# Gate and up projections of four FFN stages by seven half-width products instead of eight, with the inner layer in four parts

## The reference, cut to what matters

```python
def swiglu_2(x, w_gate_up, w_down):
    g, u = jnp.split(x @ w_gate_up, 2, axis=-1)
    return (jax.nn.silu(g) * u) @ w_down

# for i in range(2), with D_FF_2 = 2816, FFN_RES_SCALE = 0.5:
h = h + FFN_RES_SCALE * swiglu_2(rms_norm(h, ffa_norm[i]), ffa_w_gate_up[i], ffa_w_down[i])
# ... attention ...
h = h + FFN_RES_SCALE * swiglu_2(rms_norm(h, ffb_norm[i]), ffb_w_gate_up[i], ffb_w_down[i])
```

## Time and profile before

| | us |
|---|---|
| three timed runs | 3969.07, 3982.18, 3983.56 |
| median | 3982.18 |
| span of the profiled execution (the page gives no other time of it) | 3971.9 |
| PE busy | 3876.2 (98%) |
| PE weight loads busy | 3199.9 (81%) |
| DVE busy | 2080.0 (52%) |
| ACT busy | 1325.4 (33%) |
| POOL busy | 502.1 (13%) |

### The profile page before, as it was taken

One profiled execution on the slowest core, in us unless ns is written; L12 is line 12 of the kernel. 1 busy time (PEld: TensorE's weight loads), 2 busy tenths in 40 slices (PEclk: granted clock), 3 DMA queues, 4 the chain that ended last, 5 costly groups with the idle time before them and its releaser, 6 DMA issues.

```text
span 3971.9 us, 47501 instructions
## 1 busy us (share of the span) xinstructions
PE 3876.2 (98%) x19522; PEld 3199.9 (81%) x19522; DVE 2080.0 (52%) x3073; ACT 1325.4 (33%) x1977; POOL 502.1 (13%) x526
## 2 busy tenths in 40 slices
PE   8999999999999989999999989999999999999999
PEld 5788988788878878888888867888888888778887
DVE  6636566646459985333443554443643344553345
ACT  3335444322233233223322354322432233342233
POOL 0025551100012220001100143000100000010001
PEclk9999999999999999999999999999999999999999
DMA  6220003545231114233232321232322233022322
GB/s 217 85 70 1 1 1 117 159 138 182 82 101 47 61 40 137 88 104 96 94 101 80 109 64 43 96 101 83 119 87 94 94 98 97 22 64 91 106 89 70
DMA packets 342866, 350.73 MB, mean 88 GB/s; under 512 B 9595, under 2 KB 338107, under 8 KB 342396
## 3 DMA queue, kind: packets, MB, share of 16 engines
q1 hardware_dynamic: 342652, 347.70, 27.4%
HBM read 345.31 MB, written 2.10 MB: 87 GB/s over the span
## 4 chain that ended last, share of the span: by engine, by line
PE 77%; DVE 8%; ACT 1%; issue 1%; POOL 0%; DVEq 0%; ACTq 0%
PE ps L378 22%; PE ps L380 22%; PE ps L379 22%; PE ps L1576 2%; DVE wlo L360 1%; PE ps L3616 1%; PE ps L3603 1%; PE ps L3586 1%; PE ps L385 1%; PE ps L3117 1%; PE ps L2945 1%; PE ps L466 0%; PE ps L465 0%; PE ps L467 0%; DVE uv L2807 0%
## 5 line engine op out<-in xcount | busy, mean ns | idle before, releaser
L360 DVE TENSOR_TENSOR wlo<-raw,whi 128x2048 fp32r<-128x2048 f32 (+6 forms) x305 | 622.0, 2040 | 880.3 <-ACT whi L354 880.2
L378 PE MATMUL ps<-Xh,whi 128*128 128x512 f32 x2632 | 1034.2, 393 | 5.2 <-ACT cr L2707 2.5
L380 PE MATMUL ps<-Xh,wlo 128*128 128x512 f32 x2632 | 1026.2, 390 | 0.0
L379 PE MATMUL ps<-Xl,whi 128*128 128x512 f32 x2632 | 1026.0, 390 | 0.0
L354 ACT ACTIVATE whi<-raw 128x2048 fp32r<-128x2048 f32 (+6 forms) x305 | 514.5, 1687 | 1074.0 <-PE ps L380 1066.3
L378 PEld LDWEIGHTS ps<-Xh,whi 128*128 128x128 f32 x2632 | 495.1, 188 | 116.7 <-issue 13.9
L380 PEld LDWEIGHTS ps<-Xh,wlo 128*128 128x128 f32 x2632 | 495.0, 188 | 104.3
L379 PEld LDWEIGHTS ps<-Xl,whi 128*128 128x128 f32 x2632 | 495.1, 188 | 103.6 <-issue 1.4
L378 PE MATMUL ps<-HDh,whi 128*128 128x512 f32 x1056 | 411.7, 390 | 0.0
L380 PE MATMUL ps<-HDh,wlo 128*128 128x512 f32 x1056 | 410.9, 389 | 0.0
L379 PE MATMUL ps<-HDl,whi 128*128 128x512 f32 x1056 | 410.8, 389 | 0.0
(11 more groups left out here) (585 smaller groups left out, 5606.2 us busy)
## 6 DMA issues: line engine op xcount, KB each, us to landing
raw<-in_ffn_w SPq DMA_DIRECT2D x44, 1024.0 KB, 5.4
raw<-in_ffa_w_gate_up SPq DMA_DIRECT2D x44, 1024.0 KB, 5.0
raw<-in_ffb_w_gate_up SPq DMA_DIRECT2D x44, 1024.0 KB, 5.1
mslot<-in_mod_w SPq DMA_DIRECT2D x28, 1024.0 KB, 8.0
raw<-in_mod_w SPq DMA_DIRECT2D x20, 1024.0 KB, 6.0
raw<-in_ab_w_in SPq DMA_DIRECT2D x14, 1024.0 KB, 5.2
raw<-in_ffn_w SPq DMA_DIRECT2D x16, 768.0 KB, 4.4
raw<-in_hy_w_in SPq DMA_DIRECT2D x12, 1024.0 KB, 5.2
```

The costliest lines, as they stand in the source:

```text
L360: dve.tensor_tensor(k.part(k.wlo, c), k.raw(c), k.part(k.whi, c).bitcast(F32), ALU.subtract).then_inc(*k.ev.put("dve_wlo", ("lo", n), ("ra ...
L378: pe.matmul(o, wh, xh, start=first, stop=False)
L379: pe.matmul(o, wh, xl, start=False, stop=False)
L380: return pe.matmul(o, wl, xh, start=False, stop=last)
```

## The change

In a0, b0, a1 and b1, a pair of gate and up chunks is computed by a scheme of Strassen's kind. The weights of a chunk are cut into four quarters (its two halves of 128 columns, and the even and odd k-tiles), the activations also into four (even and odd k-tiles, first and last 256 tokens). Seven products of sums of quarters replace eight products of quarters. Each product is 4 k-tiles of three matmuls of 128x128 by 256 tokens, for gate and for up.

- **Weights.** Factors 0, 3 and 6 of the seven are quarters as they lie in raw; 1, 2, 4 and 5 are sums that GpSimd makes into four small buffers `stmp` (`s_ffn_pool`). Each factor is split high and low by itself, 512 columns, into a quarter of a `whi`/`wlo` buffer: eight slots, 14 factors a pair, so a factor's slot is free when the product four ahead of it has been used. The raw buffer is free behind the low split of factor 6 and GpSimd's last sum.
- **Activations.** The four sums of activation quarters, T, are made once a stage from h by VectorE (20 operations of 256 columns; `t_dve`), and split. Stage a0 does its first two pairs in the old way, the others their first one, meanwhile.
- **Results.** The products go to three PSUM banks: X (products 0, 2, 4, 6), Z (1, 5) and Y (3). Partial sums are copied out by ScalarE ("kept") and added by VectorE: C11, C22, C12. C21 is the last state of bank X. TensorE's product 6 adds to bank X and waits for C22, which reads it.
- **Parts.** The inner layer is cut into 3, 3, 3 and 2 chunks (`S_PARTS`), and each part's down projection has four chunks of weights of up to 6 k-tiles, with 8 residual updates behind it: 32 a stage instead of 16. The first down product of a part begins with the inner columns that don't come from the part's last pair.
- **Moved.** The first network's own norm, the projections of p in the b stages and a small weight's split in a1 stand at other places in the programs; the own norm's 8 updates come in one go.

```diff
+        before = max((x for x in self.holder[slot:slot + size] if x is not None), default=None)
+        u = Unit(len(self.split), c, piece, slot, before, w)
+        self.split.append(u)
+        self.holder[slot:slot + size] = [u.n] * size
...
+    def factors(self, keys):
+        for key in keys:
+            self.by[key].pieces = []
+        for i in range(7):
+            for w, key in enumerate(keys):
+                self.by[key].pieces.append(self.unit(self.by[key], i, w))
...
+S_PARTS = ((0, 0, 3), (1, 3, 3), (2, 6, 3), (3, 9, 2))
+S_FFNS = {"a0": 2, "b0": 1, "a1": 1, "b1": 1}
...
+    def s_ffn(i):
+        st, wg, wu, uoff, wd, lead = FFNS[i]
+        for part, c0, nch in S_PARTS:
+            for c in range(c0, c0 + nch):
+                plain = c < S_FFNS[st]
+                W.add((st, "g", c), wg, lead, 0, 8, c * 256, 256, plain)
+                W.add((st, "u", c), wu, lead, 0, 8, uoff + c * 256, 256, plain)
+                if not plain:
+                    W.factors([(st, "g", c), (st, "u", c)])
...
+                    W.add(("fl", 0), "od_w_in_2", (0,), 0, 8, 3072, 16, False)
...
+        if k.W.list[j - NR].pieces:
+            sp.wait_ge(*k.ev.at(("sums", j - NR)))
...
...
 def split_hi(k, act, n):
-    c = k.W.split[n]
-    act.wait_ge(*k.ev.at(("raw", c.j)))
-    if n >= NH:
-        act.wait_ge(*k.ev.at(("used", n - NH)))
-    act.activation(k.part(k.whi, c), k.raw(c), ACT.Copy).then_inc(*k.ev.put("act_whi", ("hi", n)))
+    u = k.W.split[n]
+    if u.piece is None or u.piece in DIRECT:
+        act.wait_ge(*k.ev.at(("raw", u.c.j)))
+    else:
+        act.wait_ge(*k.ev.at(("sum", u.n)))
+    if u.before is not None:
+        act.wait_ge(*k.ev.at(("used", u.before)))
+    act.activation(k.target(k.whi, u), k.source(u), ACT.Copy).then_inc(*k.ev.put("act_whi", ("hi", n)))
 def split_lo(k, dve, n):
-    c = k.W.split[n]
+    u = k.W.split[n]
     dve.wait_ge(*k.ev.at(("hi", n)))
-    dve.tensor_tensor(k.part(k.wlo, c), k.raw(c), k.part(k.whi, c).bitcast(F32), ALU.subtract).then_inc(
-        *k.ev.put("dve_wlo", ("lo", n), ("raw free", c.j)))
+    dve.tensor_tensor(k.target(k.wlo, u), k.source(u), k.target(k.whi, u).bitcast(F32), ALU.subtract).then_inc(
+        *k.ev.put("dve_wlo", ("lo", n), *([("raw free", u.c.j)] if u.piece in (None, 6) else [])))
...
+PRODUCTS = (("X", (0, 0)), ("Z", 0), ("X", 1), ("Y", (1, 0)), ("X", 2), ("Z", (1, 1)), ("X", 3))
...
+def s_pair_pe(k, pe, st, c, new):
+    ev = k.ev
+    for i, (bank, x) in enumerate(PRODUCTS):
+        ps = room(k, pe, (st, bank, c)) if i in (0, 1, 3) else k.bk.of((st, bank, c))
+        if i in (2, 4, 5):
+            pe.wait_ge(*ev.at(("kept", st, c, i)))
+        if i == 6:
+            pe.wait_ge(*ev.at(("C22", st, c)))
+        for w in range(2):
+            u = k.W[(st, "gu"[w], c)].pieces[i]
+            wh, wl, o = k.factor(k.whi, u), k.factor(k.wlo, u), ps[:, w * 256:w * 256 + 256]
+            pe.wait_ge(*ev.at(("lo", u.n)))
+            for kk in range(4):
+                if new and w == 0 and x in (0, 1, 2, 3):
+                    pe.wait_ge(*ev.at(("T", st, kk)))
+                xx = moving(k, x, kk)
+                first, last = i in (0, 1, 3) and w == 0 and kk == 0, kk == 3
+                pe.matmul(o, wh[:, kk, :], xx[:, 0, :], start=first, stop=False, skip_group_check=True)
+                pe.matmul(o, wh[:, kk, :], xx[:, 1, :], start=False, stop=False, skip_group_check=True)
+                ins = pe.matmul(o, wl[:, kk, :], xx[:, 0, :], start=False, stop=last, skip_group_check=True)
+            ins.then_inc(*ev.put("pe_ffn", ("used", u.n), *([("mm", st, i, c)] if w else [])))
...
+            pe.wait_ge(*ev.at(("lo", w.n)))
+            early = nt - 2 if cc == 0 else 0
+            for s, m in [(s, m) for s in range(2) for m in range(early)] + [(s, m) for s in range(2) for m in range(early, nt)]:
...
+def s_keep_act(k, act, st, c, i, to):
+    act.activation(to, k.bk.of((st, PRODUCTS[i][0], c))[:, :].rearrange("p (w t) -> p w t", w=2), ACT.Copy).then_inc(
+        *k.ev.put("act_keep", ("kept", st, c, {0: 2, 1: 5, 2: 4, 6: "C21"}[i]), *([("out", st, "X", c)] if i == 6 else [])))
...
+def s_pair_act(k, act, st, c, tail):
+    ev, e = k.ev, k.E[c % 2]
+    for i in range(7):
+        if tail and i < 3:
...
+        if i in (1, 2, 3):
+            act.wait_ge(*ev.at(("mm", st, i - 1, c)))
+            s_keep_act(k, act, st, c, i - 1, (e[:, 0, :, 0:256], e[:, 1, :, 256:512], e[:, 0, :, 256:512])[i - 1])
+        if i > 0:
+            for n in s_freed(k, st, c, i - 1):
+                split_hi(k, act, n)
...
+def s_add_dve(k, dve, st, c, name, bank, i, kept, e):
+    ev = k.ev
+    dve.wait_ge(*ev.at(("mm", st, i, c)))
+    dve.wait_ge(*ev.at(("kept", st, c, kept)))
+    dve.tensor_tensor(e, k.bk.of((st, bank, c))[:, :].rearrange("p (w t) -> p w t", w=2), e, ALU.add).then_inc(
+        *ev.put("dve_ffn", (name, st, c), *([("out", st, bank, c)] if bank != "X" else [])))
...
+def s_tail_dve(k, dve, st, c, at):
+    part, c0 = s_place(c)
+    m, e = 2 * (c - c0), k.E[c % 2]
+    if at == 0:
+        s_glu_dve(k, dve, st, c, 0)
+        s_scaled_dve(k, dve, st, c, 1, [("kept", st, c, "C21"), ("C22", st, c)])
+    if at == 1:
+        s_low_dve(k, dve, st, part, m, e[:, 0, 0, :])
+        s_glu_dve(k, dve, st, c, 1)
+    if at == 2:
+        s_low_dve(k, dve, st, part, m + 1, e[:, 1, 0, :])
+def s_pair_dve(k, dve, st, c, tail):
+    e = k.E[c % 2]
+    for i in range(7):
+        if i > 0:
+            for n in s_freed(k, st, c, i - 1):
+                split_lo(k, dve, n)
+        if tail and i < 3:
+            s_tail_dve(k, dve, st, c - 1, i)
+        if i == 4:
+            s_add_dve(k, dve, st, c, "C11", "Y", 3, 2, e[:, 0, :, 0:256])
+        if i == 5:
+            s_add_dve(k, dve, st, c, "C22", "X", 4, 5, e[:, 1, :, 256:512])
+        if i == 6:
+            s_add_dve(k, dve, st, c, "C12", "Z", 5, 4, e[:, 0, :, 256:512])
+            s_scaled_dve(k, dve, st, c, 0, [("C11", st, c), ("C12", st, c)])
...
+def s_ffn_pool(k, pool, st):
+    ev = k.ev
+    for c in range(S_FFNS[st], 11):
+        g, u = (k.W[(st, what, c)] for what in "gu")
+        for i in (1, 2, 4, 5):
+            for c2 in (g, u):
+                p = c2.pieces[i]
+                if i == 1:
+                    pool.wait_ge(*ev.at(("raw", c2.j)))
+                if i in (1, 2) and c > S_FFNS[st]:
+                    pool.wait_ge(*ev.at(("lo", k.W[(st, "gu"[p.w], c - 1)].pieces[i + 3].n)))
+                if i in (4, 5):
+                    pool.wait_ge(*ev.at(("lo", c2.pieces[i - 3].n)))
+                if i > 1:
+                    pool.wait_ge(*ev.at(("sum", c2.pieces[1 if i == 2 else 2].n)))
+                a, b = {1: (k.quarter(c2, 1, 0), k.quarter(c2, 1, 1)),
+                        2: (k.made(c2.pieces[1]), k.quarter(c2, 0, 0)),
+                        4: (k.quarter(c2, 1, 0), k.quarter(c2, 0, 0)),
+                        5: (k.quarter(c2, 0, 1), k.made(c2.pieces[2]))}[i]
+                pool.tensor_tensor(k.made(p), a, b, ALU.add if i == 1 else ALU.subtract).then_inc(
+                    *ev.put("pool_sum", ("sum", p.n), *([("sums", c2.j)] if i == 5 else [])))
```

359 lines of the change are left out of this document (299 added, 60 removed).

## The result

The changed kernel takes **4264.05 us** (median of 4 runs, 4257.8 to 4271.8), beside 3982.51 us of the kernel before on the same chip: ratio **1.0713**, 95% interval 1.069 to 1.0736. That is +281 us where +135 was forecast. It lies outside the range (3990 to 4180). The direction was right, the size off by a factor of two.

What follows compares the result with a forecast made beforehand. TensorE, busy 98% of the span, was taken to bound the kernel. From 3982 us, -62 saved, +140 for C22 waits with clock, and +16, +20, +13, +8 gave +135: 4117 us, range 3990 to 4180.

Steps and rivals of the forecast that it cites:

- Removed, -62: Gate and up matmuls on TensorE: seven half-width products save 1.6 us in each of 39 changed pairs, -62 us.
- Rival D: Half-width matmuls not at 0.120 us but bound by weight loads at 0.19, +400 us; chance 0.03.
- A: Rival: the products set the pace, C22 comes in time and only waits at part ends remain, 3940 us; chance 0.13.
- B: Rival: the landing loop without VectorE and GpSimd blocking each other, waits of 1.7 us, 4016 us; chance 0.25.
- VectorE and GpSimd stop each other: In changed pairs the two engines take turns on SBUF operands; one instruction of each costs 1.71 us of wall time.
- A wait of 4.4 us for C22: TensorE's seventh product waits for VectorE's addition behind the next up chunk's landing, 4.4 us, 23 times; upper end 5.6.
- The clock, 1.7 us a wait: After each of the 23 C22 waits the clock is at 0.50 for 3.4 us, losing 1.7; 6.1 a wait with it.
- (a): First changed pair of b0, a1, b1: VectorE, busy with T and other work, is 5.2 us late, +16 us.
- (b): End of a part: the last pair's chain outlasts the down matmuls that don't need it, +20 us (10 to 30).
- (d): Last part of each stage: residuals and next norm's work crowd 21.8 us of matmuls, about 2 late, +8 us.
- (c): A part's last pair: the first down chunk's split delays C22 or the part's end, +13 us (5 to 20).
- Rival C: VectorE never catches up: each wait 5.6 + 1.7 us with longer half-clock stretches, 4170 us; chance 0.17.

Runs made afterwards that it cites:

- runs 14: Kernel before with parts of 2, 3, 3, 3 in three stages and down-projection splits first, all pairs plain (no seven products): 4022.4 us.
- run 13: Changed kernel with all queue reorderings, sums on VectorE, two plain pairs heading every stage, and parts of 2, 3, 3, 3 in b0, a1, b1: 4008.9 us.
- run 10: Changed kernel with all queue reorderings and the eight sums of a pair made by VectorE instead of GpSimd: 4050.8 us.
- run 8: Four parts with all pairs plain, as in run 5, plus chunk splits moved ahead of the second gained or low part in the down projections: 4032.2 us.
- Run 2: Changed kernel with 18 unread matmuls on TensorE ahead of each of 23 waits for C22, to fill the wait: 4245.5 us.
- run 5: Changed kernel's four parts and smaller down chunks kept, but all 11 pairs of each stage plain, no sums, no T: 4041.3 us.
- Run 1: Changed kernel with VectorE's additions C11 and C22 ahead of the low split of the next pair's first up factor: 4270.3 us.
- run 9: Changed kernel with every queue reordering at once on VectorE, ScalarE and GpSimd, sums still on GpSimd: 4124.4 us.
- run 11: Changed kernel in its own old queue order, with VectorE making the eight sums of a pair instead of GpSimd: 4247.3 us.
- run 15: Version of run 13 with four edits on its remaining waits (own norm, first split, pair tails, last gained part): 3981.4 us, ratio 0.9996.

## Why the prediction was right and wrong, point by point

- **Removed, -62.** Right. Changed pairs run with starts 0.12 us apart, and the products' gain shows once most waits are gone: 13.5 us between runs 14 and 13 (run 10 was still 19 us over run 8, its plain counterpart). All 62 were never seen at once. Rival D is out, A by the 128 us of waits for C22, B by the 0.96 and 1.59 us of splits and sums.
- **"VectorE and GpSimd stop each other", 1.71 us a turn.** Right to the row: 6.88 us for four turns. By the Trainium skill ("SBUF — State Buffer", section "SBUF: two separate sides"), where whoever starts first has the port for its whole instruction, the estimate would be 4 x 1.98 = 7.9 us. The trace doesn't agree: it has 6.88.
- **A wait of 4.4 us for C22.** Right for the first transition of a part, whose 15 waits average 4.7. The 8 others take 6.7: the silu and high part of the pair before hold back the keeps in ScalarE's queue. The forecast named that as its upper end, with 1.2 us; it is 2.0 to 2.3. Together 124 us against 23 x 4.4 = 101: **+23**.
- **The clock, 1.7 us a wait.** This step failed most in size. The forecast took one stretch of 3.4 us at 0.50 from the earlier trace rows, though the 6.8 us one stood in the same rows, and put it behind the 23 waits for C22 alone. The loss is 109 - 10 = 99 against 39: **+60**. Behind those 23 waits it is 56 us, 2.4 a wait: the stretches were 6.8 us in 16 cases, 10.2 in five and 3.4 in two, but TensorE was idle in part of them. The other 43 us stand behind waits of (a), (b) and (d), which had been priced without any. Run 2 shows that most of it can't be won back alone.
- **(a) First changed pairs.** b0, a1 and b1 wait 8.5, 9.8 and 7.9 us, 26 against 16. a0, priced at nothing, waits 19 at its head and for its own norm in one lump: GpSimd's squares take turns with T there. **+29**.
- **(b) Ends of parts.** 27 against 20, in its range of 10 to 30: **+7**.
- **(c) The first down chunk's split.** 1.16 us three times, as forecast, and 0.8 in all at the four others: 4 against 13, **-9**.
- **(d) The last part.** 28 against 8: **+20**. The plain four parts (run 5) cost 58 with their clock. The forecast summed VectorE's work and called it "about 2 late"; but a down chunk of the last part is 24 matmuls, 5.4 us, which is little cover. With 36 matmuls (run 13) 19 us came back; putting the next stage's split ahead of the gained part (run 8) gave no more than 9.
- These come to +130. With the 20 us that I can't assign they are the 150 that the span (+285) has over the forecast.

**The step that failed as reasoning** is another. The forecast computed 20 x 0.55 + 8 x 1.16 = 20.3 us for a pair of 20.2 and wrote "the whole pair", and then priced only one chain, from the landing to C22, as if the rest of the time were free. Run 1 broke that chain and gained nothing, since a second one, from VectorE's splits over silu to the keep, held TensorE as long. That the turns filled the pair is not what the runs show: VectorE was idle for 22.8 of 75.5 us in a part (run 9), 9.3 of it in front of two landings. What a sum of 20.3 in 20.2 us does mean is that such idle time can't be made up. With the turns unchanged all the orders together gained 140 us (run 9); VectorE doing the sums gained 17 alone (run 11), and with the orders 213 (run 10). Rival C had the longer waits and stretches that the second transitions showed, but its name, "VectorE never catches up", and its sign, waits at L433, weren't borne out, and its 4170 was too low. How much of what the sums cost is turns, and how much is waiting for a sum on another engine, stays open: no run has the turns without the waiting.

## What to carry to other kernels

When two helpers take turns, add up their turns for one period of the loop. A sum at the period leaves nothing to make up what is lost behind a landing or in a queue, so price every chain and not only the longest. Queues in fixed order hide behind one another: mending the one whose wait showed gained nothing, two gained 28 us, all of them 140. The cheaper turn may be to let the busier engine do it all (a sum cost 0.61 us on VectorE, 1.16 us of turns on GpSimd), but only once the order is right: 17 us in the old one, 74 in the new. A new scheme also brings structure, here four parts instead of two; time it with the old arithmetic first, since it cost 58 of the 62 us that the products could win. Price a short wait of TensorE with the clock behind it, and do so for every wait of the sum: here it was 2.4 us behind a wait of 4.3 to 7.1 us.

## What was not expected of the hardware

A wait of 4.3 to 7.1 us for C22 drew the granted clock to 0.50 for 6.8 us in 16 of 23 cases. The stretch began while TensorE still waited, at 3173.1 in the first transition shown (TensorE working from 3174.75) and at 3200.4 in the second (from 3204.32). In the FFN stages of run 15 waits of 0.7 to 1.7 us drew none, and two of 2.0 us drew 3.4 us each, but one of 2.5 us drew none: the length of a wait alone doesn't settle it.

GpSimd's 512-column operation ran at 1.29 us for the first one behind a landing and at 1.7 for each that met VectorE's splits. VectorE's additions that read PSUM kept their 0.68 us in all of these runs, as in the earlier trace rows.
